# A feed-forward way up computed by feature, with one 512-column product for both parts of x and the gating on GpSimd

## The reference

```python
def swiglu(h, w1, w3, w2):
    return (jax.nn.silu(h @ w1) * (h @ w3)) @ w2
```

## Time and profile before

| | |
|---|---|
| Runs | 1427.91, 1431.92, 1434.92 us (median 1431.92) |
| Profiled execution, its own time | 1429.52 us |
| Span in the profile | 1427.7 us |
| Busy: TensorE, VectorE, ScalarE, GpSimd | 1397.6, 1014.4, 716.4, 90.3 us |
| TensorE's granted clock, mean | 0.998 of full speed |
| Data moved | 339.10 MB, 238 GB/s |

### The profile page before, as it was taken

One profiled execution on the slowest core, in us unless ns is written; L12 is line 12 of the kernel. 1 busy time (PEld: TensorE's weight loads), 2 busy tenths in 40 slices (PEclk: granted clock), 3 DMA queues, 4 the chain that ended last, 5 costly groups with the idle time before them and its releaser, 6 DMA issues.

```text
span 1427.7 us, 18521 instructions
## 1 busy us (share of the span) xinstructions
PE 1397.6 (98%) x7566; PEld 1199.3 (84%) x7566; DVE 1014.4 (71%) x1280; ACT 716.4 (50%) x927; POOL 90.3 (6%) x118
## 2 busy tenths in 40 slices
PE   9999999998999999999999999999999999999997
PEld 8788888887888878888789978788888899999886
DVE  5887677977977768877768976678746634653865
ACT  5543456456533455444565676554335544545433
POOL 1000001002000010000000352100000100000000
PEclk9999999999999999999999999999999999999999
DMA  9898865745987848888535612488755554455542
GB/s 385 353 345 295 325 232 206 311 179 199 392 318 296 317 169 317 317 312 331 199 137 188 210 71 89 177 302 335 288 194 206 184 205 157 148 175 180 193 152 112
DMA packets 50500, 339.10 MB, mean 238 GB/s; under 512 B 6720, under 2 KB 8432, under 8 KB 10352
## 3 DMA queue, kind: packets, MB, share of 16 engines
q1 hardware_dynamic: 50416, 337.92, 63.8%
HBM read 336.81 MB, written 2.66 MB: 238 GB/s over the span
## 4 chain that ended last, share of the span: by engine, by line
PE 79%; DVE 11%; ACT 4%; DMA 3%; issue 2%; POOL 1%; SPq 0%; ACTq 0%; POOLq 0%; DVEq 0%
PE ps L1020 76%; DMA raw<-units 3%; DVE wlo L1646 3%; DVE hf L2068 2%; ACT whi L553 1%; PE ps L1238 1%; DVE M L1656 1%; PE ps L1129 1%; ACT hf L634 1%; POOL ssx L470 0%; POOL base L469 0%; DVE xlo L1721 0%; DVE wlo L1651 0%; DVE unit_at L1646 0%; ACT xhi L638 0%
## 5 line engine op out<-in xcount | busy, mean ns | idle before, releaser
L1646 DVE TENSOR_TENSOR wlo<-raw,whi 128x2048 fp32r<-128x2048 f32 x212 | 486.1, 2298 | 203.4 <-ACT whi L553 203.0
L1020 PE MATMUL ps<-whi,xhi 128*128 128x512 f32 x1432 | 568.1, 397 | 7.0 <-DVE wlo L1651 1.7
L1020 PE MATMUL ps<-whi,xlo 128*128 128x512 f32 x1432 | 558.5, 390 | 0.0
L1020 PE MATMUL ps<-wlo,xhi 128*128 128x512 f32 x1432 | 558.3, 390 | 0.0
L553 ACT ACTIVATE whi<-raw 128x2048 fp32r<-128x2048 f32 x218 | 416.8, 1914 | 159.7 <-DMA raw<-units 159.6
L1020 PEld LDWEIGHTS ps<-whi,xhi 128*128 128x128 f32 x1432 | 269.2, 188 | 68.6 <-issue 4.7
L1020 PEld LDWEIGHTS ps<-whi,xlo 128*128 128x128 f32 x1432 | 269.0, 188 | 57.7
L1020 PEld LDWEIGHTS ps<-wlo,xhi 128*128 128x128 f32 x1432 | 269.5, 188 | 52.5
L1020 PE MATMUL ps<-xhi,whi 128*128 128x256 f32 x704 | 201.9, 287 | 0.1
L1020 PE MATMUL ps<-xlo,whi 128*128 128x256 f32 x704 | 199.1, 283 | 0.0
L1020 PE MATMUL ps<-xhi,wlo 128*128 128x256 f32 x704 | 199.1, 283 | 0.0
...
## 6 DMA issues: line engine op xcount, KB each, us to landing
...
```

Of the source, the lines that this page charges most:

```text
L1020: return pe.matmul(out, lhsT, rhs, start=start, stop=stop, skip_group_check=True)
L1646: dve.tensor_tensor(rest(u), landed(u), rounded(u).bitcast(F32), ALU.subtract).then_inc(w_lo, 1)
```

## The change

`xhi` and `xlo` become two halves of one array `xboth`. For blocks 2 to 10 the way up is by feature (`up_half`): the weights are the stationary operand, 128 output features q at a time, in bank 4 + q. One product of 512 columns runs the high part of the weights against both parts of x side by side (columns 0 to 255 high, 256 to 511 the rest), and one of 256 columns adds the rest of the weights against the high part of x. So a block has 32 products of 512 and 32 of 256 columns. ScalarE copies the right halves (`correction`) into SBUF, VectorE adds the left halves (`add_corrections`), ScalarE takes silu, and GpSimd multiplies and, after ScalarE's rounded copy (`product_hi`), subtracts; in block 10 VectorE does both. The values are by feature already, so these blocks need no transposes; blocks 0 and 1 keep theirs, into banks 0 and 2. The small bias product moves behind block 10 and its write into the next stage's loads. Some semaphores are shared between the two mixers. Core of the diff (semaphore names and the uses of the renamed ones left out, indentation reduced):

```diff
@@ -93,8 +93,8 @@
 whi = sb("whi", [P, NS, UNIT], F32R)
-xhi = sb("xhi", [P, 16, SEQ], F32R)
-xlo = sb("xlo", [P, 16, SEQ], F32R)
+xboth = sb("xboth", [P, 2, 16, SEQ], F32R)
+xhi, xlo = xboth[:, 0], xboth[:, 1]
 WORDS = 16384
@@ -172,6 +172,7 @@
 g = [m(12800, T, FB), m(13312, T, FB)]
+gate_sum, up_sum = g
 cb = m(15360, D)
@@ -368,9 +369,6 @@
     gate_out(n)
-    if n == 0:
-        sp.wait_ge(S["wd_ok"], 1)
-        sp.dma_start(scratch[:, :], wdist[0:H_AT, :]).then_inc(S["scratch_out"], 16)
 if i == 9:
@@ -383,6 +381,9 @@
     load(u0 + u)
+if u == 4:
+    sp.wait_ge(S["wd_ok"], 1)
+    sp.dma_start(scratch[:, :], wdist[0:H_AT, :]).then_inc(S["scratch_out"], 16)
 if u == 6:
@@ -527,6 +528,16 @@
 else:
+    if kind == "ffn":
+        b, nine = NF * FFN_NO[n], (NF - 2) * FFN_NO[n]
+        for i in range(2, NF - 1):
+            pool.wait_ge(S["up_sum"], 2 * (nine + i - 1))
+            pool.wait_ge(S["up_sil"], nine + i - 1)
+            pool.tensor_tensor(up_sum, gate_sum, up_sum, ALU.mult).then_inc(S["up_g"], 1)
+            pool.wait_ge(S["gt_hi"], b + i + 1)
+            j = 8 + 2 * (i % 4)
+            pool.tensor_tensor(xlo[:, j:j + 2, :], up_sum, xhi[:, j:j + 2, :].bitcast(F32),
+                               ALU.subtract).then_inc(S["gt_lo"], 1)
     if n == 0:
@@ -702,19 +713,31 @@
 if kind == "ffn":
-    b = NF * FFN_NO[n]
+    b, two, nine = NF * FFN_NO[n], 2 * FFN_NO[n], (NF - 2) * FFN_NO[n]
-        if b + i:
-            act.wait_ge(g_ok[t], b + i)
+        if two + i:
+            act.wait_ge(g_ok[t], two + i)
         else:
...
     def gated_hi(i):
-        act.wait_ge(S["gt_ps"], b + i + 1)
-        act.activation(xhi[:, 8 + 2 * (i % 4):10 + 2 * (i % 4), :], ps[:, 6, :], ACT.Copy)\
+        act.wait_ge(S["gt_ps"], two + i + 1)
+        act.activation(xhi[:, 8 + 2 * i:10 + 2 * i, :], ps[:, 2 * i, :], ACT.Copy)\
+           .then_inc(S["gt_hi"], 1)
+    def correction(dst, bank):
+        act.activation(dst, ps[:, bank:bank + 2, SEQ:512], ACT.Copy).then_inc(S["up_corr"], 1)
+    def silu_sum(i):
+        act.wait_ge(S["up_sum"], 2 * (nine + i - 2) + 1)
+        act.activation(gate_sum, gate_sum, ACT.Silu).then_inc(S["up_sil"], 1)
+    def product_hi(i):
+        act.wait_ge(S["up_g"], nine + i - 1)
+        act.activation(xhi[:, 8 + 2 * (i % 4):10 + 2 * (i % 4), :], up_sum, ACT.Copy)\
            .then_inc(S["gt_hi"], 1)
@@ -722,14 +745,20 @@
     hi(a + 3)
-    gated_hi(i - 1)
+    if i == 2:
+        gated_hi(1)
     hi(a + 4)
-    act.wait_ge(s1_ok, (NF - 2) * FFN_NO[n] + i - 1)
-    silu(i, 0, 4)
+    act.wait_ge(s1_ok, nine + i - 1)
+    correction(gate_sum, 4)
     wait_used(act, a + 1)
-    silu(i, 1, 5)
+    act.wait_ge(S["gt_lo"], b + i)
+    correction(up_sum, 6)
+    silu_sum(i)
+    if i == NF - 1:
+        product_hi(i)
     hi(a + 5)
-gated_hi(NF - 1)
+    if i < NF - 1:
+        product_hi(i)
 hi(u0 + 34)
@@ -1226,46 +1255,63 @@
 if kind == "ffn":
-    b = NF * FFN_NO[n]
+    b, two, nine = NF * FFN_NO[n], 2 * FFN_NO[n], (NF - 2) * FFN_NO[n]
...
         for t in range(T):
-            pe.wait_ge(g_ok[t], b + i + 1)
-        if b + i:
-            pe.wait_ge(S["gt_lo"], b + i)
+            pe.wait_ge(g_ok[t], two + i + 1)
         for kk in range(2):
             for t in range(T):
-                r = pe.transpose(ps[:, 6, kk * SEQ + t * P:kk * SEQ + (t + 1) * P],
-                                 g[i % 2][:, t, kk * P:(kk + 1) * P], ident[:, :])
+                r = pe.transpose(ps[:, 2 * i, kk * SEQ + t * P:kk * SEQ + (t + 1) * P],
+                                 g[i][:, t, kk * P:(kk + 1) * P], ident[:, :])
         r.then_inc(S["gt_ps"], 1)
+    def up_free(i, q):
+        if i == 2:
+            pe.wait_ge(g_ok[q // 2], two + q % 2 + 1)
+        elif q % 2 == 0:
+            pe.wait_ge(S["up_sum"], 2 * (nine + i - 3) + q // 2 + 1)
+    def up_half(i, half):
+        u = up_unit(n, i, half)
+        ready(u)
+        for q in range(4):
+            if half == 0:
+                up_free(i, q)
+            both = ps[:, 4 + q, :].rearrange("p (a b) -> p a b", b=SEQ)
+            for kk in range(4):
+                k = 4 * half + kk
+                w = slice(kk * 512 + q * P, kk * 512 + q * P + P)
+                mm(both, rounded(u)[:, w], xboth[:, :, k, :], start=(k == 0))
+                r = mm(ps[:, 4 + q, 0:SEQ], rest(u)[:, w], xhi[:, k, :], stop=(k == 7))
+            if half and q == 1:
+                r.then_inc(s1_ok, 1)
+        r.then_inc(w_used, 1)
...
     for i in range(2, NF):
-        a = up_unit(n, i, 0)
-        pe.wait_ge(g_ok[0], b + (i if i > 2 else 1))
-        by_token(a, 0, 0, 4)
-        pe.wait_ge(g_ok[i > 2], b + i)
-        by_token(a, 0, 1, 5).then_inc(w_used, 1)
-        if i > 2:
-            turn(i - 1)
-        by_token(a + 1, 1, 0, 4).then_inc(s1_ok, 1)
+        up_half(i, 0)
         if i == 2:
             turn(1)
-        by_token(a + 1, 1, 1, 5).then_inc(w_used, 1)
-        if n == 0 and i == 5:
-            pe.wait_ge(S["bias_in"], 48)
-            mm(ps[0:H_AT, 7, 0:REL], rel_sb[0:32, :], oneh_sb[0:32, :], start=True, stop=True)\
-                .then_inc(S["wd_ps"], 1)
+        up_half(i, 1)
         j = i - 2
...
         down(d, 8 + 2 * (j % 4), 0, start=(j == 0))
+        if j == 0:
+            pe.wait_ge(S["gt_lo"], b + 2)
         if i < NF - 1:
             down(d, 8 + 2 * (j % 4), 1, start=(j == 0)).then_inc(w_used, 1)
-    turn(NF - 1)
+    if n == 0:
+        pe.wait_ge(S["bias_in"], 48)
+        pe.wait_ge(S["up_sum"], 2 * (NF - 3) + 1)
+        mm(ps[0:H_AT, 4, 0:REL], rel_sb[0:32, :], oneh_sb[0:32, :], start=True, stop=True)\
+            .then_inc(S["wd_ps"], 1)
     last = [(down_unit(n, j), 8 + 2 * (j % 4)) for j in range(NF - 3, NF)]
@@ -1844,22 +1890,37 @@
 if kind == "ffn":
-    b = NF * FFN_NO[n]
+    b, two, nine = NF * FFN_NO[n], 2 * FFN_NO[n], (NF - 2) * FFN_NO[n]
     v = ADA_FIRST[n]
-        dve.wait_ge(sil_ok[t], b + i + 1)
-        if t == 0 and i >= 2:
-            dve.wait_ge(S["gt_ps"], b + i - 1)
-        dve.tensor_tensor(g[i % 2][:, t, :], sil[:, t, :], ps[:, bank, FB:2 * FB], ALU.mult)\
+        dve.wait_ge(sil_ok[t], two + i + 1)
+        dve.tensor_tensor(g[i][:, t, :], sil[:, t, :], ps[:, bank, FB:2 * FB], ALU.mult)\
            .then_inc(g_ok[t], 1)
...
         dve.wait_ge(S["gt_hi"], b + i + 1)
+        j = 8 + 2 * i
+        dve.tensor_tensor(xlo[:, j:j + 2, :], ps[:, 2 * i, :].rearrange("p (a b) -> p a b", b=SEQ),
+                          xhi[:, j:j + 2, :].bitcast(F32), ALU.subtract).then_inc(S["gt_lo"], 1)
+    def add_corrections(i):
+        for j, total in enumerate((gate_sum, up_sum)):
+            dve.wait_ge(S["up_corr"], 2 * (nine + i - 2) + j + 1)
+            dve.tensor_tensor(total, ps[:, 4 + 2 * j:6 + 2 * j, 0:SEQ], total, ALU.add)\
+               .then_inc(S["up_sum"], 1)
+    def product(i):
+        dve.wait_ge(S["up_sum"], 2 * (nine + i - 1))
+        dve.wait_ge(S["up_sil"], nine + i - 1)
+        dve.tensor_tensor(up_sum, gate_sum, up_sum, ALU.mult).then_inc(S["up_g"], 1)
+    def product_lo(i):
+        dve.wait_ge(S["gt_hi"], b + i + 1)
         j = 8 + 2 * (i % 4)
-        dve.tensor_tensor(xlo[:, j:j + 2, :], ps[:, 6, :].rearrange("p (a b) -> p a b", b=SEQ),
-                          xhi[:, j:j + 2, :].bitcast(F32), ALU.subtract).then_inc(S["gt_lo"], 1)
+        dve.tensor_tensor(xlo[:, j:j + 2, :], up_sum, xhi[:, j:j + 2, :].bitcast(F32),
+                          ALU.subtract).then_inc(S["gt_lo"], 1)
@@ -1881,13 +1942,13 @@
     ada(v)
-gated_lo(i - 1)
-if i > 2:
-    lo(a + 4)
-gate_up(i, 0, 4)
-gate_up(i, 1, 5)
 if i == 2:
-    lo(a + 4)
+    gated_lo(1)
+lo(a + 4)
+add_corrections(i)
+if i == NF - 1:
+    product(i)
+    product_lo(i)
 lo(a + 5)
@@ -1895,11 +1956,10 @@
         gate_columns(0)
-    if n == 0 and i == 5:
-        dve.wait_ge(S["wd_ps"], 1)
-        dve.tensor_tensor(wdist[0:H_AT, :], ps[0:H_AT, 7, 0:REL], negr_sb[0:H_AT, :], ALU.add)\
-           .then_inc(S["wd_ok"], 1)
-gated_lo(NF - 1)
+if n == 0:
+    dve.wait_ge(S["wd_ps"], 1)
+    dve.tensor_tensor(wdist[0:H_AT, :], ps[0:H_AT, 4, 0:REL], negr_sb[0:H_AT, :], ALU.add)\
+       .then_inc(S["wd_ok"], 1)
 ada_done(v - 1)
```

34 lines of the change are left out of this document (17 added, 17 removed).

## The result

The changed kernel takes 1441.76 us (median of 5 executions, 1438.55 to 1444.17) against 1431.39 for the kernel before (5 executions, 1427.91 to 1434.92): a ratio of 1.0068, 95% interval 1.0052 to 1.0083. It is 10.4 us slower where 3.5 us less was forecast, and just outside the range of 1420 to 1441.

What follows compares the result with a forecast made beforehand. Inside a block only TensorE's own work was taken to count, VectorE next to bind. The terms -7.6 - 1.0 + 1.0 + 3.6 + 0.5 gave -3.5 us, a median of 1428.4, range 1420 to 1441.

Steps and rivals of the forecast that it cites:

- The up pair: Up products of blocks 2 to 10: a 512- plus a 256-column product takes 0.346 us, 0.20 more a block.
- the first rival: Up products: each 512 behind a 256 keeps a long step, 0.0135 us more a pair, +15.6, 1444; chance 0.24.
- The turns that left TensorE: Blocks 2 to 9: seven transposes of 0.50 us leave TensorE's path, 3.5 us a stage; net of dearer pairs -7.6.
- The end of a stage: Feed-forward stage ends: x turned 0.9 us later, +3.6 over four, 0.5 more in the first; TensorE stands about 2.5.
- U + 10.5: Stage end: U is when block 10's up products end; VectorE was forecast to start the gated y 10.5 us later.
- The start of the first stage: First new block: TensorE waits for the last gate product, which VectorE finishes at 57.05; +1.0 us, wait of 1.5.
- GpSimd: Product and subtraction in eight blocks a stage: length costs nothing, some 80 us more busy; about one operation meets VectorE's subtraction.
- VectorE's round: Rival, inner blocks: VectorE's work from one gate sum to the next, 14.6 us, becomes the bound; +28, 1456; chance 0.09.
- the end of the stage did not stay short: Rival, stage ends: they are not lengthened, so the +4.1 falls away, 1424.3 us; chance 0.15.
- weight loads: Rival, up pairs: loads not hidden under 120 ns make a pair cost two 512 products, +123, 1552; chance 0.02.

Runs made afterwards that it cites:

- Runs of sixteen and of four: Changed kernel with up products ordered as sixteen (or four) 512-column products, then as many 256-column ones, instead of alternating: 1436.74 us (sixteen), 1436.17 us (four).
- the operand in one piece: Changed kernel whose 512-column products read two neighbouring tiles of the rounded x, lying in one piece, instead of one tile's rounded part and rest: 1441.24 us.
- e_dve_product: Changed kernel with the product of the gated values and their rest on VectorE in all blocks, nothing on GpSimd in the loop: 1441.36 us.
- e_runs16: Changed kernel with all sixteen 512-column up products of each half first, the sixteen 256-column ones behind them: 1436.74 us, ratio to the kernel before 1.0039.
- e_tail2: Changed kernel with half the outside unit's rest moved behind the gated y at the feed-forward stage's end, into VectorE's waits for the roots: 1437.16 us.

## Why the prediction was wrong, point by point

**The up pair: the step that failed at full clock.** "... so in alternation the two should mostly cancel. I take 0.346." It is 0.353: 7 ns x 1152 pairs = 8 us. With it the forecast of 3.5 less becomes 4.5 more; the dearer down products behind each block's pairs make another 2, and 5 to 6.6 more at full clock is what the runs have. The mechanism was the first rival's, a 512 behind a 256 keeps a long step; its price was 0.0135 and half of that holds, since the 256 behind a 512 gives back 3 ns of 10. I had read a seam that is crossed once, by starts rounded to 10 ns, and where cheap and dear ends were 15.6 us apart that rounding was the whole question. Runs of sixteen and of four, against the operand in one piece, show it.

**The turns that left TensorE** (7 x 0.50 a stage) did leave: with runs of sixteen the block is 16.58 where 16.81 and 16.51 stood, and the stages are 1.3 us below the kernel before. The forecast was 3.5 below; 1.4 of the difference is the pair, still 0.3472 on average over the halves there, and 1.4 the longer wait for the last gate product, which is this order's own.

**The end of a stage** was right: the gated y at U + 10.5, a longer stand before each turn (forecast about 2.5, measured 1.47 to 2.67). **What such a stand does was missed.** I priced it by its length. The granted clock also fell to half for 3.4 us at two of the four turns, each time at a cost of 1.2 us more; filling the stands gave 3.8 us back in the median. In the kernel before longer stands came with 2.2 us more counted as lost, the mLSTM stage's part in it. This is the second step that failed, and it was in no rival.

**The start of the first stage:** TensorE stands 1.40 us for the last gate product, forecast 1.5.

**GpSimd:** at no cost on the path, as forecast, by e_dve_product. Its size was off: 1.30 us for the product and 2.89 for the rest, 138 us more busy time and not 80. Nor was the stretched VectorE instruction the subtraction, which stays at a mean of 2297 ns; it is the first ada column behind it (2.31 instead of 1.22; mean 1417 against 1219).

**Rivals.** VectorE's round did not become the bound, the end of the stage did not stay short, and weight loads stay hidden.

**What stays open.** The part of the clock's share that the fills at the turns don't give back (by the table some 1.5 us): above all the two stretches of 6.8 us in the Mamba stage, whose code the change doesn't touch, where the trace before has one of 3.4. In the profiled execution they weigh more than the turns do: from the sixteen transposes in that stage (at 807.02 and 798.20) to the turn of x at its end it is 126.8 us after and 122.4 before, 4.4 more. They come and go between traces (e_runs16 has none there and takes 121.2, e_tail2 has two of 3.4), and no run here settles what sets them. Why a product behind one of another length takes longer wasn't tried beyond the three orders.
